# Query projection in two token halves, with each head's first selection behind its chunk, its low weight parts on GpSimd, and weight-matrix slots in tile order

## The chip, the core and the metric

One core of a Trainium2 chip runs the kernel as one program. The metric is device time in microseconds (us). The engines are PE (TensorE: matmuls), ACT (ScalarE: activations, copies out of PSUM), DVE (VectorE), POOL (GpSimd) and SP (SyncE, which only issues DMAs here). Each runs its own instruction list in order and meets the others at semaphores.

## The reference

A decoder layer for 512 tokens of width 1024. Only its last part, PEER (product-key expert retrieval), is touched. `hf` is the normed stream, 512 x 1024.

```python
q = (hf @ w_query).reshape(T, PEER_HEADS, 2, PEER_HALF)           # 8 heads, two halves of 128
s = jnp.einsum('thpd,pkd->thpk', q, sub_keys)                     # 128 sub-keys per half
sv, si = lax.top_k(s, PEER_TOPK)                                  # first selection: 16 of 128
cand = sv[..., 0, :, None] + sv[..., 1, None, :]                  # 16 x 16 sums
top_s, top_pos = lax.top_k(cand, PEER_TOPK)                       # second selection
idx = take_along_axis(cand_idx, top_pos)                          # 8 x 16 experts of 16384 per token
g = softmax(top_s)
out = sum over the 128 (t, k):  g * gelu(hf[t] . down[idx]) * up[idx]
```

The result, times a gate, is added to the stream and normed once more.

## The kernel before

All matmul weights arrive as chunks of 256 output columns (1 MB) in three raw slots. Each chunk is split into a high part (`whi`, ACT, `whi_make`) and a low part (`wlo`, raw minus high, DVE, `wlo_make` in `follow`), each in two buffers, and PE makes three products of 512 columns per k-tile: 48 matmuls per chunk. `CHUNKS` is the hand-written order. The last stage is `query`, eight chunks, one per head.

The PEER part serves its tokens in two ways. Token blocks 0 and 1 (`GB` = 2) **gather**: for each of 256 (block, k) pairs POOL issues an indirect DMA that brings one row of `down` per token (512 KB) into a ring, DVE multiplies it with `h2row` and sums (a **dot**, function `dots`; 256 of them, ring of 4), and later POOL gathers the rows of `up` and DVE adds them, scaled, to `accum` (a **sum**; 256, ring of 8). Token blocks 2 and 3 go **dense**: PE multiplies all 128 tiles of `downT` by the tokens (the **first stream**, `i` in `range(ET)`), ACT applies Gelu to each result and stores it in `wmat`; DVE and PE then build the gate matrix from one-hot vectors and multiply it into `wmat` (the **weighing**, 64 steps of `one_hots` and `weigh`); PE multiplies `wmat` by all 128 tiles of `up` (the **second stream**). SP feeds both streams through the ring `stream`.

DVE's own list sets the order of the rest. After the query stage it runs `route(n)` for the four token blocks: 16 first selections (`top16` over `s_all`), pairing, 8 second selections, decoding of positions with six 2048-wide one-hot operations. From block 1 on it mixes dots between these. Then, in this order:

```python
            for b in range(DB):
                softmax(GB + b).then_inc(pick_ready, 1)
            for b in range(GB):
                softmax(b)
            dots(P, P)
            dve.drain()
            dve.sem_inc(pre_ready, 1)
            dots(DOTS_FIRST)
```

`dots(P, P)` ends block 0's 128 dots, `DOTS_FIRST` more follow from block 1, and only then come the weighing, the remaining dots and the sums. `softmax(n)` waits for `exp_done`, which ACT gives in its loop over the first stream: at `i == EXP_AT` (100), behind the Gelu of 100 tiles, it makes the exponentials. The kernel after the last sum scales, norms and stores the output.

Of the kernel before, what the change touches and what calls it, by code (L numbers as in the profile page):

```python
# [26 lines left out]
SLOT0 = 18  # L27
# [5 lines left out]
DOTS_FIRST = 40  # L33
# [7 lines left out]
C_ID, C_ROT, C_MASK, C_FREQ, C_INV, C_IOTA, C_IOTAW = 0, 128, 256, 384, 385, 401, 529  # L41
C_W = 529 + 128
# [6 lines left out]
          ("gateB", 4), ("branchA", 4), ("out", 4), ("query", 8))  # L49
# [52 lines left out]

def tile_plan():


    tiles = []
    for s, c in CHUNKS:
        if (s, c) == ("query", 0):
            tiles += [("x1tok", n, "act") for n in range(8)]
        if (s, c) == ("query", 4):  # L110
            tiles += [("h2tok", n, "act") for n in range(2 * GB)]
            tiles += [("gaterow", n, "dve") for n in range(2)]
# [7 lines left out]
    tiles += [("score", n, "act") for n in range(16)]  # L120
    return tiles
# [25 lines left out]


def wslot(i):

    return (i + SLOT0) % ET


def layer(nc, consts, chans, rows, xT_d, pos_d, subk_d, ada_d, wdram, downT, down, up, x1d, gated, out):
# [4 lines left out]
    with ExitStack() as ctx:  # L159
# [85 lines left out]
        sq2 = place("sq2", [P, KT, S], f32, 164)  # L245
# [7 lines left out]
        q2T = place("q2T", [P, 2 * PH, S], f32, 68)  # L253

        wmat = place("wmat", [P, ET, DT], f32, 12)
        s_all = place("s_all", [P, TB, 2 * PH, NKEYS], f32, 100)
        s_left = place("s_left", [P, 2 * PH, NKEYS], f32, 132)
        cand_left = place("cand_left", [P, PH, PAIRS], f32, 132)
        onehot = place("onehot", [P, PH, TOPK, TOPK], f32, 12)
        at = [20.0]  # L260

        def scratch(name, shape, dt=f32, upto=30):
# [5 lines left out]
        top_v = scratch("top_v", [P, PH, 2, TOPK])  # L268
        top_i = scratch("top_i", [P, PH, 2, TOPK], u32)
        top_f = scratch("top_f", [P, PH, 2, TOPK])  # L270
# [5 lines left out]
        start_f = place("start_f", [P, 2, PH, TOPK], f32, 136)  # L276
# [6 lines left out]
        gate_row = place("gate_row", [P, D], f32, 192)  # L283
# [13 lines left out]
        x1stage = place("x1stage", [P, TB, D], f32, 164)  # L297
        x1tok = place("x1tok", [P, TB, D], f32, 30)
        yrow = place("yrow", [P, TB, D], f32, 46)
        gate_fin = place("gate_fin", [P, D], f32, 62)  # L300
        gain_row = place("gain_row", [P, D], f32, 66)
        junk = place("junk", [P, D], f32, 70)
# [51 lines left out]
        h2_ready = sem("h2_ready")  # L354
# [40 lines left out]
        N_OP = dict(norm1=0, pooled=8, ya=16, o=24, merged=32, norm2=40)  # L395
        N_MEAN = dict(norm1=0, norm2=1)
# [3 lines left out]
        def _(sp):  # L400
# [3 lines left out]
            for n, item in enumerate(STREAM):  # L404
                if n >= RAW_SLOTS:
                    sp.wait_ge(raw_free, n - RAW_SLOTS + 1)
# [9 lines left out]
                if item == ("w", FIRST["query"]):  # L416
                    sp.wait_ge(ada_done, 6)
                    sp.dma_start(bias_row[:, :], rows[:, D:2 * D]).then_inc(row_in, 16)
                if item == ("w", FIRST["query"] + 5):
# [6 lines left out]
            wait_emptied(sp, "gaterow", 1)  # L426
            sp.dma_start(gated, gate_row[:, :]).then_inc(gate_stored, 16)

            sp.wait_ge(x1_stored, 16)
            for n in range(2 * ET):  # L430
# [3 lines left out]
                sp.dma_start(stream[:, n % RING, :], src).then_inc(stream_in[n % RING], 16)  # L434
                if n == ET + 64:
                    sp.dma_start(x1tok[:, :, :], x1d).then_inc(fin_in, 16)
# [9 lines left out]
        def _(pe):  # L446
# [135 lines left out]

            t = 0
            for n, (stage, c) in enumerate(CHUNKS):
# [5 lines left out]
                if stage == "query" and c == 0:  # L590
                    norm2_mean()
                    t = tokens_first(t, x1T, range(8))
                if stage == "query" and c == 4:
                    pe.wait_ge(h2_ready, 8)
                    t = tokens_first(t, h2T, range(2 * GB))
                    for m in range(2):
                        free_bank(t)
                        pe.matmul(bank[:, BANK[t], :], ones[:, :], acc_ada[:, 1, m * S:(m + 1) * S],
                                  start=True, stop=True).then_inc(tile_ready, 1)
                        t += 1  # L600
                if c == 0:
                    ready = {"xp": "norm1", "pool": "pooled", "branchP": "ya",
                             "out": "merged", "query": "norm2"}.get(stage)
                    if ready:
# [4 lines left out]
                ah, al = {"pool": (r1_hi, r1_lo), "branchP": (ya_hi, ya_lo), "branchA": (r1_hi, r1_lo),  # L609
                          "query": (r1_hi, r1_lo)}.get(stage, (hT_hi, hT_lo))  # L610
# [21 lines left out]
                else:  # L632
                    for m in range(2):
                        free_bank(t)
                        for k in range(KT):
                            if WOVEN <= n < WOVEN_END and k % 4 == 0:
                                woven(4 * (n - WOVEN) - 12 + 2 * m + k // 4)
                            if stage == "branchA" and c == 0 and m == 0:
                                pe.wait_ge(alo_ready, N_OP["o"] + k + 1)
                            last = mm3(bank[:, BANK[t], :], wh[:, k, m * P:(m + 1) * P],  # L640
                                       wl[:, k, m * P:(m + 1) * P], ah[:, k, :], al[:, k, :],
                                       k == 0, k == KT - 1)
                        last.then_inc(tile_ready, 1)
                        t += 1

            for n in range(16):
                tb, g = n // 4, n % 4
                free_bank(t)
                if n == 0:
                    pe.wait_ge(pos_in, 48)  # L650
                    wait_emptied(pe, "query", 15)
                for j in range(4):
                    hp = 4 * g + j
                    last = pe.matmul(bank[:, BANK[t], j * P:(j + 1) * P], q2T[:, hp, tb * P:(tb + 1) * P],
                                     subk[:, hp % 2, :], start=True, stop=True)
                last.then_inc(tile_ready, 1)
                t += 1
# [38 lines left out]
            for i in range(ET):  # L696
                stream_tile(ET + i)
                for tb in range(DB):
                    for half in range(2):
                        last = pe.matmul(bank[:, 2 * tb + half, :], wmat[:, wslot(i), tb * P:(tb + 1) * P],  # L700
# [14 lines left out]
        def _(act):  # L715
# [137 lines left out]

            for n, (stage, c) in enumerate(CHUNKS):
# [30 lines left out]
                elif stage == "out":  # L885
                    if c == 3:
                        root(N_MEAN["norm2"], 1.0 / D)
                        for k in range(8):
                            act.activation(x1stage[:, k // 2, (k % 2) * S:(k % 2 + 1) * S],
                                           tile("x1tok", k), ACT.Copy).then_inc(act_emptied, 1)  # L890
                        for k in range(KT):
                            act.wait_ge(part_ready, 24 + k + 1)
                            act.activation(r1_hi[:, k, :], h2T[:, k, :], ACT.Identity,
                                           bias=modc[:, 24 + k:25 + k]).then_inc(ahi_ready, 1)
                elif stage == "query":
                    if c == 4:
                        for k in range(2 * GB):
                            act.activation(h2row[:, k // 2, (k % 2) * S:(k % 2 + 1) * S],
                                           tile("h2tok", k), ACT.Copy).then_inc(act_emptied, 1)
                    for m in range(2):  # L900
                        act.activation(q2T[:, 2 * c + m, :], tile(stage, 2 * c + m), ACT.Copy)\
                           .then_inc(act_emptied, 1)
            for n in range(16):
                tb, g = n // 4, n % 4
# [644 lines left out]
```

## Time and profile before

| quantity | value |
|---|---|
| median of 3 runs | 1987.07 us (1982.69 to 1989.71) |
| profiled execution: time / span of the core | 1997.52 / 1995.7 us |
| busy PE / DVE / ACT / POOL | 1633.1 / 1381.3 / 322.7 / 544.4 us |
| chain that ended last, share of the span | DVE 37%, DMA 30%, PE 22% |
| costliest lines of the chain | gathers of `down` 18%, gathers of `up` 10%, sums 10% |
| PE matmul of the first stream (L678) / second stream (L700) | 444.3 / 444.2 us busy |
| dots (L1269) / sums (L1428) on DVE | 311.6 / 328.8 us busy, 256 each |
| landing of a gather of `down` / of `up`, median | 7.4 / 7.1 us |
| bytes over the span | 489.76 MB, mean 245 GB/s |

PE has the most busy time, but its streams stand between stretches of DVE and gathers, so shares of the whole span do not say which one ends last; the stretches do.

### The profile page before, as it was taken

What the parts mean: (1) busy time and instruction counts of PE and PEld (TensorE: products, weight loads), DVE (VectorE), ACT (ScalarE), POOL (GpSimd) and SP (SyncE); (2) the same over time, 40 slices, a digit from 0 to 9 for tenths busy, and PEclk for the clock granted to TensorE, in tenths of its full rate; (3) what the DMA queues carried; (4) which work ended last, traced back from release to release, by engine and by line L of the source; (5) the groups of instructions that cost most, each with busy time, mean ns of one, the idle gap of its engine ahead of it and who ended that gap; (6) DMA issues with size and microseconds to landing.
All of it is one profiled execution on the core that took longest, in us unless ns stands there. A gap on an engine that the chain in (4) does not pass through costs nothing.

```text
span 1995.7 us, 18994 instructions
## 1 busy us (share of the span) xinstructions
PE 1633.1 (82%) x6668; PEld 1191.1 (60%) x6668; DVE 1381.3 (69%) x2790; ACT 322.7 (16%) x658; POOL 544.4 (27%) x516
## 2 busy tenths in 40 slices
PE   2798999989997999999999967789999899980000
PEld 1686877767776788888888866654444344430000
DVE  5656456666554268899888579985555566679998
ACT  2242244436413221111111100000000000000001
POOL 0000000000000003353444420014444544457773
PEclk7899999989998999999999986669999899995555
DMA  7323311132423228999998960019999999999995
GB/s 292 140 92 147 127 64 64 64 127 106 169 95 106 74 72 311 356 365 375 353 369 322 386 253 0 1 52 392 376 374 375 412 409 409 410 409 388 367 384 230
DMA packets 123070, 489.76 MB, mean 245 GB/s; under 512 B 13792, under 2 KB 14048, under 8 KB 113632
## 3 DMA queue, kind: packets, MB, share of 16 engines
q0 software_dynamic: 73728, 268.47, 35.2%
q1 hardware_dynamic: 49248, 220.09, 29.3%
q8 instruction: 53, 0.87, 0.2%
q14 instruction: 41, 0.34, 0.1%
HBM read 483.78 MB, written 4.72 MB: 245 GB/s over the span
## 4 chain that ended last, share of the span: by engine, by line
DVE 37%; DMA 30%; PE 22%; issue 3%; DVEq 3%; ACT 2%; POOL 2%; SPq 0%; ACTq 0%; POOLq 0%
DMA ring<-in_down,idx 18%; DMA ring<-in_up,idx 10%; DVE accum L1428 10%; PE bank L449 6%; PE bank L450 6%; PE bank L451 6%; DVE ring L1269 6%; DVE h2T L1398 3%; DVE h2T L1397 2%; DVE wmat L1408 2%; POOL ring L1453 2%; DVE acc_ada L956 1%; DMA raw<-in_ada 1%; DVE onehot L1352 1%; PE bank L535 1%
## 5 line engine op out<-in xcount | busy, mean ns | idle before, releaser
L1453 POOL DMA_INDIRECT ring<-in_down,idx x256 | 278.8, 1089 | 1249.8 <-DVE idx L1360 759.7
L700 PE MATMUL bank<-stream,wmat 128*128 128x512 f32 x1024 | 444.2, 597 | 9.1 <-DMA stream<-in_up 8.3
L678 PE MATMUL bank<-h2T,stream 128*128 128x256 f32 x2048 | 444.3, 380 | 2.6 <-ACT wmat L930 2.6
L1269 DVE CUSTOM_DVE_ANT_0 ring<-ring,h2row 128x1024 f32<-128x1024 f32 x256 | 311.6, 1222 | 167.2 <-DMA ring<-in_down,idx 164.1
L678 PEld LDWEIGHTS bank<-h2T,stream 128*128 128x128 f32 x2048 | 390.1, 191 | 56.2 <-issue 3.0
L1428 DVE SCALAR_TENSOR_TENSOR accum<-ring,share,accum 128x1024 f32<-128x1024 f32 x256 | 328.8, 1284 | 107.6 <-DMA ring<-in_up,idx 94.1
L700 PEld LDWEIGHTS bank<-stream,wmat 128*128 128x128 f32 x1024 | 196.0, 192 | 256.7 <-issue 246.5
L1453 POOL DMA_INDIRECT ring<-in_up,idx x256 | 265.4, 1037 | 172.5 <-DVE accum L1428 119.2
L449 PE MATMUL bank<-hT_hi,whi 128*128 128x512 f32 x384 | 160.9, 419 | 23.5 <-DVE hT_lo L1006 17.0
L975 DVE TENSOR_TENSOR wlo<-raw,whi 128x2048 fp32r<-128x2048 f32 x45 | 103.0, 2290 | 108.4 <-ACT whi L722 108.0
L690 PE MATMUL bank<-h2T 128*128 128x128 f32 x512 | 114.1, 393 | 49.9 <-DVE h2T L1398 49.9
L450 PE MATMUL bank<-hT_lo,whi 128*128 128x512 f32 x384 | 153.0, 398 | 0.0
L451 PE MATMUL bank<-hT_hi,wlo 128*128 128x512 f32 x384 | 152.4, 397 | 0.0
L690 PEld LDWEIGHTS bank<-h2T 128*128 128x128 f32 x512 | 97.8, 285 | 66.4 <-DVE h2T L1398 66.3
L930 ACT ACTIVATE wmat<-bank 128x256 f32<-128x256 f32 x128 | 49.0, 384 | 392.2 <-PE bank L678 383.7
L449 PEld LDWEIGHTS bank<-hT_hi,whi 128*128 128x128 f32 x384 | 74.0, 193 | 42.0 <-DVE hT_lo L1006 17.1
L722 ACT ACTIVATE whi<-raw 128x2048 fp32r<-128x2048 f32 x45 | 86.1, 1912 | 79.8 <-PE bank L451 68.9
L449 PE MATMUL bank<-r_hi,whi 128*128 128x512 f32 x208 | 83.5, 402 | 18.3 <-DVE r_lo L1006 10.0
L450 PEld LDWEIGHTS bank<-hT_lo,whi 128*128 128x128 f32 x384 | 74.2, 193 | 17.2 <-issue 2.9
L1398 DVE TENSOR_SCALAR h2T<-cst,ijT,gT 128x128 f32<-128x128 f32 x256 | 84.3, 329 | 0.0
L451 PEld LDWEIGHTS bank<-hT_hi,wlo 128*128 128x128 f32 x384 | 74.1, 193 | 16.4
L450 PE MATMUL bank<-r_lo,whi 128*128 128x512 f32 x208 | 82.7, 397 | 0.0
(201 smaller groups left out, 1596.8 us busy)
## 6 DMA issues: line engine op xcount, KB each, us to landing
stream<-in_downT SPq DMA_DIRECT2D x128, 512.0 KB, 6.5
stream<-in_up SPq DMA_DIRECT2D x128, 512.0 KB, 6.8
raw<-in_ada SPq DMA_DIRECT2D x24, 1024.0 KB, 6.0
raw<-in_w_query SPq DMA_DIRECT2D x8, 1024.0 KB, 4.9
raw<-in_w_xp SPq DMA_DIRECT2D x4, 1024.0 KB, 6.0
raw<-in_w_gateA SPq DMA_DIRECT2D x4, 1024.0 KB, 4.9
raw<-in_w_branchP SPq DMA_DIRECT2D x4, 1024.0 KB, 4.8
raw<-in_w_q SPq DMA_DIRECT2D x4, 1024.0 KB, 4.8
```

What stands on the lines that cost most here:

```text
L449: pe.matmul(dst, lhi, rhi, start=first, stop=False)
L450: pe.matmul(dst, lhi, rlo, start=False, stop=False)
L451: return pe.matmul(dst, llo, rhi, start=False, stop=last)
L678: last = pe.matmul(bank[:, 4 + i % 2, 0:DT], stream[:, i % RING, k * P:(k + 1) * P], h2T[:, k, GB * P:S], start=(k == 0), stop=(k == KT - 1))
L690: last = pe.matmul(bank[:, 6 + par, n * P:(n + 1) * P], h2T[:, 4 * par + n, 0:P], h2T[:, 4 * par + n, P:2 * P], start=True, stop=True)
L700: last = pe.matmul(bank[:, 2 * tb + half, :], wmat[:, wslot(i), tb * P:(tb + 1) * P], stream[:, (ET + i) % RING, half * S:(half + 1) * S], ...
L722: act.activation(whi[:, n % 2], raw_w(n), ACT.Copy).then_inc(hi_ready, 1)
L975: dve.tensor_tensor(wlo[:, n % 2], raw_w(n), whi[:, n % 2].bitcast(f32), ALU.subtract)\
L1269: dve.tensor_tensor_reduce(out=ring[g % RING][:, :], in0=ring[g % RING][:, :], in1=h2row[:, b, :], scale=1.0, scalar=0.0, op0=ALU.mult, op ...
L1398: last = dve.tensor_scalar(h2T[:, 4 * par + n, P:2 * P], iota_w, ijT[:, b, 0, t:t + 1], gT[:, b, t:t + 1], ALU.is_equal, ALU.mult)
L1428: dve.scalar_tensor_tensor(accum[:, b, :], ring[slot][:, :], share[:, b, k:k + 1], accum[:, b, :], ALU.mult, ALU.add).then_inc(sum_done, 1)
L1453: pool.indirect_dma_start(out=ring[slot][:, :], out_offset=None, in_=table, in_offset=bass.IndirectOffsetOnAxis(ap=idx[:, b, k:k + 1], axi ...
```

## The change

The query stage becomes two stages, `queryA` (tokens 0 to 255) and `queryB` (256 to 511), of eight chunks each; each loads and splits the same eight weight chunks again. A matmul has 256 columns instead of 512. The scores of a head follow one chunk later (`score`), ACT copies them out, and DVE makes that head's first selection (`stage1`: 2 token blocks x 2 halves). Pairing, second selection and decoding of a token block are `stage2`. The low parts of these 16 chunks are made by POOL, in its list ahead of all gathers. The second norm is made in halves, with the shift on ACT; transposes for the stored stream and the gate row move into the `out` stage and between the chunks. `q2T` now holds two heads, `s_all` one half's scores. `wmat` is filled in tile order (`wslot` goes), `DOTS_FIRST` goes from 40 to 64, and the dots mixed into the routing are dealt by `fill`, one per 1.4 us of credit.

```diff
-DOTS_FIRST = 40
+DOTS_FIRST = 64
+ROUTE_PER_DOT = 1.4
-          ("gateB", 4), ("branchA", 4), ("out", 4), ("query", 8))
+          ("gateB", 4), ("branchA", 4), ("out", 4), ("queryA", 8), ("queryB", 8))
...
+            def score(t, u):
+                c = u % 8
+                free_bank(t)
...
+                wait_emptied(pe, "queryB" if u >= 8 else "queryA", 2 * c + 1)
+                for tb in range(2):
+                    for m in range(2):
+                        last = pe.matmul(bank[:, BANK[t], (2 * tb + m) * P:(2 * tb + m + 1) * P],
+                                         q2T[:, c % 2, m, tb * P:(tb + 1) * P], subk[:, m, :],
...
+            def shifted(half):
+                toks = slice(half * HT, (half + 1) * HT)
+                for k in range(KT):
+                    act.wait_ge(part_ready, 24 + half * KT + k + 1)
+                    act.activation(hT_hi[:, k, toks], h2T[:, k, toks], ACT.Identity, bias=modc[:, 24 + k:25 + k])
+                    act.activation(h2T[:, k, toks], h2T[:, k, toks], ACT.Identity,
+                                   bias=modc[:, 24 + k:25 + k]).then_inc(ahi_ready, 1)
...
                 if i == PICK_AT + 1:
                     for b in range(DB):
                         pick_out(b)
-                if 70 <= i < 70 + 8 * TB and i % 8 == 6:
-                    act.wait_ge(logit_ready, (i - 70) // 8 + 1)
-                if i == 102:
-                    act.wait_ge(pick_ready, DB)
+                if i == 88:
+                    act.wait_ge(routes_done, 1)
...
-                if n >= len(CHUNKS):
+                if n >= QUERY:
                     return
                 wlo_make(n)
...
+            def fill(us):
+
+                credit[0] += us
+                while credit[0] >= ROUTE_PER_DOT:
+                    credit[0] -= ROUTE_PER_DOT
+                    dots(1, P)
...
-            for n in range(TB):
-                for g in range(4):
-                    wait_emptied(dve, "score", 4 * n + g)
-                route(n, 1 if n else 0)
+            for c in range(PH):
+                stage1(0, c, nothing)
+            stage2(0, nothing)
+            stage2(1, fill)
+            for c in range(PH):
+                stage1(1, c, fill)
+            for n in range(GB, TB):
+                stage2(n, fill)
+            dve.sem_inc(routes_done, 1)
...
-            pool.wait_ge(gate_stored, 16)
+            for n in range(QUERY, len(CHUNKS)):
+                pool.wait_ge(lo_ready, n)
+                pool.wait_ge(hi_ready, n + 1)
+                pool.tensor_tensor(wlo[:, n % 2].rearrange("p a b -> p (a b)"),
+                                   raw_w(n).rearrange("p a b -> p (a b)"),
+                                   whi[:, n % 2].bitcast(f32).rearrange("p a b -> p (a b)"), ALU.subtract)\
+                    .then_inc(lo_ready, 1)
+                pool.drain()
+                pool.sem_inc(qraw_free, 1)
+
+            pool.wait_ge(x1_stored, 16)
```

POOL's list before, from the first gather on:

```order
L1453 DMA ring<-in_down,idx 128x1024 [waits idx_ready,gate_stored]
L1453 DMA ring<-in_down,idx 128x1024 x3
L1453 DMA ring<-in_down,idx 128x1024 [waits dot_done] x124
L1453 DMA ring<-in_down,idx 128x1024 [waits dot_done,idx_ready]
L1453 DMA ring<-in_down,idx 128x1024 [waits dot_done] x127
```

and after:

```order
L1553 TENSOR_TENSOR wlo<-raw,whi 128x2048 [waits hi_ready,lo_ready] x16
L1545 DMA ring<-in_down,idx 128x1024 [waits idx_ready,x1_stored]
L1545 DMA ring<-in_down,idx 128x1024 x3
L1545 DMA ring<-in_down,idx 128x1024 [waits dot_done] x124
L1545 DMA ring<-in_down,idx 128x1024 [waits dot_done,idx_ready]
```

Sixteen subtractions now stand ahead of the first gather, each behind its chunk's high part.

ACT's list from the end of the query stage to the copies of the picks (`ijT`), before; `wmat` is a Gelu of the first stream, `share` and `picked` are the exponentials:

```order
L901 ACTIVATE q2T<-bank 128x512 [waits tile_ready] x4
L905 ACTIVATE s_all<-bank 128x512 [waits tile_ready] x16
L930 ACT_TABLE_LOAD
L930 ACTIVATE wmat<-bank 128x256 [waits tile_used] x70
L930 ACTIVATE wmat<-bank 128x256 [waits tile_used,logit_ready]
...
L911 ACT_TABLE_LOAD
L911 ACTIVATE share<-share 128x128 [waits logit_ready] x2
L911 ACTIVATE picked<-picked 128x128 [waits logit_ready] x2
L930 ACT_TABLE_LOAD
L930 ACTIVATE wmat<-bank 128x256 [waits tile_used] x2
L930 ACTIVATE wmat<-bank 128x256 [waits tile_used,pick_ready]
```

and after:

```order
L959 ACTIVATE q2T<-bank 128x256 [waits tile_ready] x2
L906 ACTIVATE s_all<-bank 128x512 [waits s1_done,tile_ready] x2
L985 ACT_TABLE_LOAD
L985 ACTIVATE wmat<-bank 128x256 [waits tile_used] x88
L985 ACTIVATE wmat<-bank 128x256 [waits tile_used,routes_done]
L985 ACTIVATE wmat<-bank 128x256 [waits tile_used] x11
L968 ACT_TABLE_LOAD
L968 ACTIVATE share<-share 128x128 [waits logit_ready] x2
L968 ACTIVATE picked<-picked 128x128 [waits logit_ready] x2
L985 ACT_TABLE_LOAD
L985 ACTIVATE wmat<-bank 128x256 [waits tile_used] x9
```

The exponentials keep their place behind 100 Gelus; the wait on the routing stands at tile 88, and the one on `pick_ready` behind them is gone.

On DVE the dots can be counted in the two lists (one `ring,pre<-ring,h2row` each): before, 126 stand ahead of the first softmax and 42 between the softmaxes and the weighing; after, 89 and 103. The dots behind the weighing go from 88 to 64.

## Rows read from the trace of the kernel before

**Rows 1.** View of windows, all engines, from the first gather to the end.

```profile
core 0: us, PE busy (x) PEld busy (x) DVE busy (x) ACT busy (x) POOL busy (x), PEclk, DMA share, GB/s
...
760.00:1080.00 320.00, 320.00 (x1485) 281.69 (x1484) 281.98 (x906) 38.68 (x98) 142.05 (x129) 1.00 0.96 360
...
1178.00:1334.00 156.00, 114.23 (x513) 97.90 (x513) 153.94 (x575) 0.00 (x0) 1.46 (x2) 0.65 0.03 8
...
1786.00:1990.00 204.00, 0.41 (x1) 0.00 (x0) 187.98 (x149) 6.18 (x10) 140.70 (x131) 0.51 0.90 346
```

**Rows 2.** Timeline of ACT (ScalarE) around its hundredth weight tile.

```profile
1067.22 0.38 ACT L930 ACTIVATE wmat<-bank 128x256 f32<-128x256 f32 x1 [3.07 <-PE bank L678]
...
1069.84 1.28 ACT L930 ACT_TABLE_LOAD   x1
```

**Rows 3.** Timeline of DVE (VectorE) at the end of the routing.

```profile
1081.28 0.28 DVE L1368 TENSOR_REDUCE expsum<-picked 128x8 f32<-128x128 f32 x1
...
1084.63 1.22 DVE L1269 CUSTOM_DVE_ANT_0 ring<-ring,h2row 128x1024 f32<-128x1024 f32 x1
```

**Rows 4.** Timeline of DVE where the weighing begins.

```profile
1176.49 1.23 DVE L1269 CUSTOM_DVE_ANT_0 ring<-ring,h2row 128x1024 f32<-128x1024 f32 x1 [0.20 <-DMA ring<-in_down,idx]
...
1177.64 0.28 DVE L1397 TENSOR_SCALAR h2T<-cst,ijT 128x128 f32<-128x128 f32 x1
```

**Rows 5.** View of windows, instructions on the gather ring alone.

```profile
1080.00:1178.00 98.00, 52.53 (x43) 42.59 (x43) 0.96 0.97 367
1334.00:1440.00 106.00, 57.28 (x47) 51.83 (x46) 0.99 0.95 361
1548.00:1786.00 238.00, 146.60 (x115) 113.07 (x117) 0.98 1.03 410
```

**Rows 6.** Timeline of DVE just after the last matmul of the weight stream.

```profile
1783.07 17.81 DVE L1428 SCALAR_TENSOR_TENSOR accum<-ring,share,accum 128x1024 f32<-128x1024 f32 x13
```

**Rows 7.** View of DMA issues from 1790 to 1974, us to landing.

```profile
ring<-in_up,idx POOLq DMA_INDIRECT x128, 6.0
```

**Rows 8.** Timeline of PE (TensorE), two neighbouring matmuls of 256 columns.

```profile
304.08 0.28 PE L451 MATMUL bank<-whi,hT_lo 128*128 128x256 f32 x1
304.20 0.28 PE L449 MATMUL bank<-whi,hT_hi 128*128 128x256 f32 x1
```

**Rows 9.** Timeline of PE before and after the score matmuls.

```profile
707.32 14.53 PE L654 MATMUL bank<-subk,q2T 128*128 128x128 f32 x128 [0.78 <-ACT q2T L901]
721.68 4.48 PE L678 MATMUL bank<-h2T,stream 128*128 128x256 f32 x20
```

**Rows 10.** Timeline of ACT in the query projection.

```profile
607.48 1.92 ACT L722 ACTIVATE whi<-raw 128x2048 fp32r<-128x2048 f32 x1
619.96 0.60 ACT L901 ACTIVATE q2T<-bank 128x512 f32<-128x512 f32 x1 [10.57 <-PE bank L451]
```

**Rows 11.** Timeline of DVE from the second norm into the query projection.

```profile
597.70 3.35 DVE L997 RECIPROCAL rms<-rms 128x512 f32<-128x512 f32 x1 [1.89 <-ACT rms L733]
601.12 5.39 DVE L1243 SCALAR_TENSOR_TENSOR h2T<-x1T,scaleF,rms 128x512 f32<-128x512 f32 x8
...
627.84 2.29 DVE L975 TENSOR_TENSOR wlo<-raw,whi 128x2048 fp32r<-128x2048 f32 x1 [10.66 <-ACT whi L722]
```

**Rows 12.** Timeline of DVE in the first routing.

```profile
711.89 3.19 DVE L1278 MAX8 top_v<-s_all 128x8 f32<-128x128 f32 x16 [22.35 <-ACT s_all L905]
...
731.30 0.29 DVE L1337 CAST top_f<-top_i 128x256 f32<-128x256 uint32 x1
...
758.92 0.29 DVE L1360 SCALAR_TENSOR_TENSOR idx<-rowij 128x128 int32<-128x128 f32 x1
```

**Rows 13.** Timeline of POOL (GpSimd), gathers of `down`.

```profile
760.13 1.07 POOL L1453 DMA_INDIRECT ring<-in_down,idx  x1 [759.68 <-DVE idx L1360]
...
843.75 1.68 POOL L1453 DMA_INDIRECT ring<-in_down,idx  x1 [7.63 <-DVE pre L1269]
...
850.43 0.94 POOL L1453 DMA_INDIRECT ring<-in_down,idx  x1 [0.30 <-issue]
```

More of the change, by code:

```diff
@@ L26 @@
 ET = 128
-SLOT0 = 18
 RING = 4
@@ L32 @@
 PICK_AT = 108
-DOTS_FIRST = 40
+DOTS_FIRST = 64
+ROUTE_PER_WLO = 4.0
+ROUTE_PER_DOT = 1.4
+HALF = {"queryA": 0, "queryB": 1}
+HT = S // 2
 NEG = -3.0e38
@@ L107, in tile_plan @@
     for s, c in CHUNKS:
-        if (s, c) == ("query", 0):
-            tiles += [("x1tok", n, "act") for n in range(8)]
-        if (s, c) == ("query", 4):
+        if (s, c) == ("out", 1):
+            tiles += [("gaterow", n, "dve") for n in range(2)]
+        if (s, c) == ("out", 3):
+            tiles += [("x1tok", 2 * n, "act") for n in range(4)]
+        if (s, c) == ("queryA", 1):
+            tiles += [("x1tok", 2 * n + 1, "act") for n in range(4)]
+        if (s, c) == ("queryA", 3):
             tiles += [("h2tok", n, "act") for n in range(2 * GB)]
-            tiles += [("gaterow", n, "dve") for n in range(2)]
         if s == "pool":
@@ L119, in tile_plan @@
             tiles += [(s, 2 * c + n, who) for n in range(2)]
-    tiles += [("score", n, "act") for n in range(16)]
+        if s in HALF and (s, c) != ("queryA", 0):
+            tiles.append(("score",) + score_before(s, c) + ("act",))
+    tiles.append(("score", 15, "act"))
     return tiles
@@ L589, in _ @@
                         o_columns(h)
[L590 to L595, printed above, removed]
+                if (stage, c) == ("out", 1):
                     for m in range(2):
                         free_bank(t)
+                        if m == 0:
+                            pe.wait_ge(ada_acc, 6)
                         pe.matmul(bank[:, BANK[t], :], ones[:, :], acc_ada[:, 1, m * S:(m + 1) * S],
@@ L644, in _ @@
                         t += 1
[L646 to L657, printed above, removed]
+                    if stage in HALF and (stage, c) != ("queryA", 0):
+                        t = score(t, *score_before(stage, c))
+            t = score(t, 15)
             def stream_tile(n):
@@ L699, in _ @@
                     for half in range(2):
-                        last = pe.matmul(bank[:, 2 * tb + half, :], wmat[:, wslot(i), tb * P:(tb + 1) * P],
+                        last = pe.matmul(bank[:, 2 * tb + half, :], wmat[:, i, tb * P:(tb + 1) * P],
                                          stream[:, (ET + i) % RING, half * S:(half + 1) * S],
@@ L884, in _ @@
                         act.activation(hT_hi[:, i, :], tmpo[:, i, :], ACT.Copy).then_inc(ahi_ready, 1)
[L885 to L896, printed above, removed]
+                elif stage == "out" and c == 3:
+                    for k in range(0, 8, 2):
+                        x1_out(k)
+                    root(N_MEAN["norm2"], 1.0 / D)
+                    shifted(0)
+                elif stage in HALF:
+                    if (stage, c) == ("queryA", 1):
+                        shifted(1)
+                        for k in range(1, 8, 2):
+                            x1_out(k)
+                    if (stage, c) == ("queryA", 3):
                         for k in range(2 * GB):
+                            if k == 0:
+                                act.wait_ge(part_ready, 24 + 2 * KT)
                             act.activation(h2row[:, k // 2, (k % 2) * S:(k % 2 + 1) * S],
@@ L900, in _ @@
                     for m in range(2):
-                        act.activation(q2T[:, 2 * c + m, :], tile(stage, 2 * c + m), ACT.Copy)\
+                        if c >= 2 or stage == "queryB":
+                            act.wait_ge(tile_ready, TILE_AT["score", 8 * HALF[stage] + c - 2] + 1)
+                        act.activation(q2T[:, c % 2, m, :], tile(stage, 2 * c + m)[:, 0:HT], ACT.Copy)\
                            .then_inc(act_emptied, 1)
-            for n in range(16):
-                tb, g = n // 4, n % 4
-                act.activation(s_all[:, tb, 4 * g:4 * g + 4, :].rearrange("p a b -> p (a b)"),
-                               tile("score", n), ACT.Copy).then_inc(act_emptied, 1)
+                    if (stage, c) != ("queryA", 0):
+                        score_out(*score_before(stage, c))
+            score_out(15)
             def exponentials(n):
@@ L1279, in top16 @@
                     if n % 4 == 3:
-                        dots(among)
+                        fill(0.8)
                 dve.drain()
```

226 lines of the change are left out of this document (140 added, 86 removed).

## The prediction, made before the changed kernel ran

> **What bounds the kernel now.** I read the view of windows first [rows 1]. From 760 to 1080 PE and the gathers run together, and the DMA engines are 96% busy at 360 GB/s; so it goes on to 1178 [rows 5]. From 1178 to 1334 only the weighing runs: DVE is busy 153.94 of 156 us, the DMA engines rest at 0.03, PE has a mean granted clock of 0.65. PE's last matmul ends near 1786, and 204 us of sums and output follow in which PE does nothing. So the end is set by DVE's own list, and PE matters only through where the weighing starts, since the second stream follows it. Then I read what DVE does at three places. Its softmaxes begin at 1081.28 and the next dot at 1084.63 [rows 3]. ACT has its hundredth Gelu at 1067.22 and goes back to Gelu at 1069.84, with the exponentials made [rows 2]. So the routing ended some 11 us after its exponentials: DVE did not wait for them. The weighing begins at 1177.64 [rows 4], after 42 more dots.
>
> **The rates.** Beside a stream the ring of 4 gives 43 dots in 98 us, 2.28 each, and 47 records in 106 us after the weighing, 2.26 each [rows 5]; I take 2.3 there. Sums beside the stream: 115 in 238 us, 2.07 each [rows 5]. With the stream over: 13 sums in 17.81 us, 1.37 each [rows 6]. PE's stream: first matmul at 721.68 [rows 9], hundredth Gelu at 1067.22 [rows 2], so 3.455 us a tile and 442 us for 128.
>
> **The change, part by part.**
>
> *Query stage.* Two matmuls of 256 columns are 0.12 us apart [rows 8], so a chunk takes 48 x 0.12 = 5.8 us. The 64 score matmuls took 14.53 us [rows 9], four are 0.9. PE alone would need 6.7 us a chunk. But the splitting makes a loop over two chunks: when a chunk's matmuls end, ACT has to copy its queries and, once the four score matmuls are through (0.9), the scores (0.6, as a copy of 512 columns [rows 10]; with wakes 0.8), then makes the high part (1.92 [rows 10]), POOL makes the low part (P), and the matmuls of the chunk after next follow (5.8). Period (0.9 + 0.8 + 1.9 + 0.3 + P + 5.8) / 2 = (9.7 + P) / 2.
>
> *P.* No POOL arithmetic is in the trace. DVE needs 2.29 us for the same subtraction [rows 11], which is the lower end, and there PE's 6.7 is the period. POOL's own instructions stretch from 0.94 to 1.68 us when DVE is at work [rows 13]. I take twice the DVE time, 4.6, a period of 7.15; for the upper end four times, 9.2, a period of 9.45. The Trainium skill, GPSIMD Engine Reference, section "Elementwise — side-by-side cycle accounting", gives 4497 ns for this size on GpSimd against 2293 on VectorE; the trace agrees with the second, the first would make the period 7.1 and move nothing.
>
> *Start.* Half the transposes of the stored stream (16) and the two gate-row products move ahead of the norm: at 0.23 us each, and four times that for 512 columns, 5.4 us. The reciprocal that began at 597.70 [rows 11] begins at 603.1; its half takes 1.7, the first part 0.34, and ACT then makes two 256-column results per k-tile, 0.38 each (as in [rows 2]), so chunk 0 ends at about 614.6. Chunk 1 needs banks that ACT frees only after two high parts, 16 shifts of 0.38 and a copy: about 624, end 629.8. Chunk 2 ends at 636.5, chunk 3, behind four row copies, at 646.4. Twelve more at 7.15 end at 732, and after the last scores the first stream starts at 734, against 721.68: **12 us late**.
>
> *First gather.* `idx` of block 0: the scores of head 7 of the first half come out at about 684; 16 first selections took 711.89 to 731.30, so four take 4.85, and the rest of a route took 731.30 to 758.92 plus 0.3 [rows 12], 27.9. That gives 717. But POOL does its sixteenth subtraction first, done when the last chunk's matmuls start, 726. The gather starts there, **34 us sooner** than 760.13 [rows 13]. The stored stream's DMA, issued in `queryA`, is long done. DVE meets its first mixed dot right after 717 and waits for it till 733.
>
> *Routing.* Before, three routes with 42 dots each filled 1081.3 - 760.1 = 321 us, 107 each; less 19.4 + 27.9 of routing that is 1.42 us per mixed dot. After: three second stages of 27.9, eight first ones of 4.85, 89 dots of 1.42: 249 us. Routing ends at 982.
>
> *The wait that is new.* The exponentials still stand behind 100 Gelus: 734 + 345.5 + 2.6 = 1082. So DVE, which reached them 11 us late, comes **100 us early** and stands still with four gathered rows in the ring. Behind the waiting softmax stand 103 dots, where 42 stood, then the weighing, and behind that PE's second stream, and the last 64 dots and all sums. `DOTS_FIRST` = 64 adds 24 of these dots, and the thinner mixing 37.
>
> *Start of the weighing.* Softmaxes end at 1086, the first stream at 734 + 442 = 1176. In these 90 us go 4 ready dots (5 us) and 85 / 2.28 = 37. The other 62 have the DMA engines to themselves. Their price isn't in the trace. Lower end: DVE's own spacing, 1.15 us, from 1176.49 to 1177.64 [rows 4]; upper end: 2.28. With the ring of 8 and no stream a gather landed in 6.0 us [rows 7], queued behind seven others, at 1.37 a sum; with 4 in flight the round (issue 1.2, landing 4 to 5, dot 1.2) gives about 1.6. I take 1.6: 99 us. The weighing starts at 1275, against 1177.6: **97 us late**. Its own 156 us and PE's stream keep their lengths, so PE ends 97 us late too.
>
> *After it.* 24 fewer dots at 2.3 give 55 us back. In these, 55 / 2.07 = 27 more sums are made before PE ends, and each spares 1.37 us behind it: 37 us back. The slots of `wmat` and the one iota instead of two change no instruction and no size in the weighing: nothing.
>
> *Sum.* The span 1995.7 + 97 - 37 = 2056. The profiled execution's time was 1997.52, 10.4 above the median of 1987.07; so against the median, 1987 + 60 = **2047**.
>
> **A rule weighed.** POOL's gather instruction took 1.68 us instead of 0.94 at 843.75 [rows 13], while DVE worked on two-input operations. The Trainium skill, GPSIMD Engine Reference, section "Key points", says that POOL shares its SBUF interfaces with VectorE and contends with instructions that have two SBUF inputs. By that rule the low parts beside DVE's decoding (about 14 us of one-hot work in `queryB`) would take longer, some 5 us in all; without it, none.
>
> **The rivals.**
> 1. *The wait costs more: the dots keep their price.* If the ring of 4, not the stream, sets 2.28, the 62 dots cost 141 us, and the time is 2089. For it: landing was still 6.0 us without a stream [rows 7]. Against: DVE took 1.37 per sum there. 12%.
> 2. *POOL becomes the bound of the query stage.* At P = 9.2, twelve periods of 9.45 instead of 7.15 delay everything by 28 us: 2075. For it: the stretch in [rows 13]; against: DVE mostly waits or has one-input selections in that stage. 13%.
> 3. *The other side: faster.* The dots behind the softmax run at DVE's own pace. From 1086, 103 at 1.15 end at 1204; the weighing is then 27 us late, the 37 given back outweigh it: 1977. It decides from 1214 on, that is 1.24 us a dot. Against: beside the stream two stretches gave 2.28 and 2.26 [rows 5], with the DMA engines at 97%; this needs both to be wrong. 4%.
> 4. *The change doesn't do what it says:* the early selection gains nothing, because the first gather waits for POOL's queue till 760 as before. The routing would then end at 1016, still before 1082, and the time would be the same 2047. It is no case of its own; it shows how little the early start is worth while 1082 stands.
>
> **How the numbers follow.** Main case 71%, with its own range from all 62 dots at 1.15 (2019) to 2.28 less a little (2080). Rivals 1 and 2 make 25% between 2065 and 2095, rival 3 4%. The range 2015 to 2092 leaves out rival 3 and the sum of rivals 1 and 2. 0.3% (6 us) is about what this measurement can tell from no change. Faster 4%; within 0.3% needs 1.3 us a dot in all stretches, 2%; slower 94%.
>
> **What would show it.** In the profile after: first stream at about 734, first gather near 726, last mixed dot near 980; then DVE idle for some 100 us, put down to ACT's exponentials (or a DMA); PE idle between 1176 and 1275, DMA lighter there, granted clock down; weighing 156 us long; PE's end near 1883; then about 110 sums at 1.37. Wrong would be: a softmax that starts with no wait before it, or a PE gap below 40 us ahead of the weighing.

## The result, and the profile after

The changed kernel takes 2081.38 us (median of 4 runs, 2075.61 to 2082.82), against 1988.39 for the kernel before: ratio 1.0468, 95% interval 1.0438 to 1.0498. It is 93 us slower. The ratios here and below leave out slow executions; the only one, 3378.58 us, is among e9's twelve, whose median without it is 1990.36. The profiled execution of the changed kernel has a span of 2080.3 us, 84.6 more than the span before.

The view of windows, all engines; the cuts are the end of the routing, the end of the first stream and the weighing:

```profile
core 0: us, PE busy (x) PEld busy (x) DVE busy (x) ACT busy (x) POOL busy (x), PEclk, DMA share, GB/s
740.00:988.00 248.00, 248.00 (x1151) 218.86 (x1150) 221.43 (x705) 28.69 (x73) 113.52 (x92) 1.00 0.95 343
988.00:1088.00 100.00, 100.00 (x465) 88.26 (x464) 0.80 (x5) 13.91 (x35) 0.94 (x1) 1.00 0.48 169
1088.00:1183.00 95.00, 94.13 (x440) 82.74 (x438) 51.39 (x90) 12.57 (x34) 44.06 (x39) 1.00 0.95 355
1183.00:1307.00 124.00, 3.09 (x14) 3.07 (x15) 82.42 (x145) 0.00 (x0) 79.17 (x64) 0.51 0.83 282
1307.00:1463.00 156.00, 118.32 (x507) 99.20 (x507) 154.06 (x564) 0.00 (x0) 1.32 (x1) 0.63 0.00 1
```

Two stretches have no counterpart in [rows 1, 5]. From 988 to 1088 DVE is busy for 0.80 us of 100, and the DMA engines fall to 0.48, since no gather is asked for. From 1183 to 1307 PE is busy for 3.09 us of 124. The weighing behind them has kept its length. The view of waits names the first stretch, and PE's second:

```profile
DVE ring L1327 <- DMA ring<-in_down,idx: 162.1, 156, 4.2
PE bank L721 <- DVE h2T L1490: 158.7, 63, 121.8
DVE expsum L1455 <- ACT picked L968: 99.1, 1, 99.1
```

Each line gives the total us, how often, and the longest single wait: DVE waited once, 99.1 us, for ACT's exponentials (`picked`), and PE's longest wait, 121.8 of its 158.7 us, was for the one-hot vectors that DVE makes at the start of the weighing. Against [rows 2, 3], the timelines of ACT and DVE around the exponentials and at the weighing:

```profile
1084.82 0.39 ACT L985 ACTIVATE wmat<-bank 128x256 f32<-128x256 f32 x1 [3.07 <-PE bank L709]
...
1087.44 1.28 ACT L985 ACT_TABLE_LOAD   x1
```

```profile
986.97 1.22 DVE L1327 CUSTOM_DVE_ANT_0 ring<-ring,h2row 128x1024 f32<-128x1024 f32 x1
...
1087.25 0.28 DVE L1455 TENSOR_REDUCE expsum<-picked 128x8 f32<-128x128 f32 x1 [99.05 <-ACT picked L968]
...
1300.80 1.23 DVE L1327 CUSTOM_DVE_ANT_0 ring<-ring,h2row 128x1024 f32<-128x1024 f32 x1 [0.22 <-DMA ring<-in_down,idx]
1301.95 0.28 DVE L1489 TENSOR_SCALAR h2T<-cst,ijT 128x128 f32<-128x128 f32 x1
```

The last mixed dot begins at 986.97, the softmax at 1087.25, the weighing at 1301.95, 124 us behind [rows 4].

The view of windows on the gather ring alone, in the three stretches with dots and the last one with sums (the columns are DVE's dots or sums, then POOL's gathers, then clock, DMA share and GB/s):

```profile
740.00:988.00 248.00, 107.13 (x89) 113.52 (x92) 1.00 0.95 343
1088.00:1183.00 95.00, 48.92 (x40) 44.06 (x39) 1.00 0.95 355
1183.00:1305.00 122.00, 77.31 (x63) 79.17 (x64) 0.51 0.83 281
...
1900.00:2060.00 160.00, 145.91 (x114) 114.92 (x107) 0.55 0.96 368
```

63 dots with no stream beside them took the 119 us from 1183 to 1302: 1.89 each. The DMA view gives 5.6 us from issue to landing there.

The start of the gathers, POOL and DVE:

```profile
712.71 4.69 POOL L1553 TENSOR_TENSOR wlo<-raw,whi 128x2048 fp32r<-128x2048 f32 x1 [2.74 <-ACT whi L753]
719.54 4.83 POOL L1553 TENSOR_TENSOR wlo<-raw,whi 128x2048 fp32r<-128x2048 f32 x1 [2.14 <-ACT whi L753]
726.96 4.60 POOL L1553 TENSOR_TENSOR wlo<-raw,whi 128x2048 fp32r<-128x2048 f32 x1 [2.59 <-ACT whi L753]
740.07 1.10 POOL L1545 DMA_INDIRECT ring<-in_down,idx  x1 [8.51 <-DVE idx L1447]
```

```profile
705.59 4.47 DVE L1399 TENSOR_SCALAR best_f<-best_sh 128x128 f32<-128x128 uint32 x1
...
713.03 4.52 DVE L1412 TENSOR_TENSOR best_f<-best_f,start_f 128x128 f32<-128x128 f32 x1
717.62 2.29 DVE L1434 TENSOR_TENSOR h2T<-best_f,cst 128x2048 f32<-128x2048 f32 x1
719.99 6.53 DVE L1439 TENSOR_TENSOR h2T<-h2T,top_f 128x2048 f32<-128x2048 f32 x1
726.59 2.29 DVE L1443 TENSOR_REDUCE rowij<-h2T 128x128 f32<-128x2048 f32 x1
728.95 4.76 DVE L1434 TENSOR_TENSOR h2T<-best_f,cst 128x2048 f32<-128x2048 f32 x1
...
738.86 0.29 DVE L1447 SCALAR_TENSOR_TENSOR idx<-rowij 128x128 int32<-128x128 f32 x1
```

Read the two together. The operation at 719.99 takes 2.29 us where no subtraction of POOL runs (e6 below shows the same line of the kernel); here it ends at 726.52, 2.15 after POOL's subtraction from 719.54 to 724.37 has ended. The subtraction of 128 columns at 713.03 ends at 717.55, behind POOL's at 717.40. The reduction at 726.59 runs beside POOL's next subtraction, from 726.96 on, and isn't held. So block 0's second stage, from 694.77 to 739.15, took 44.4 us instead of 27.9.

### The profile page after: what moved, and what is told of

Read it like the earlier page. It is cut to its first block, busy times and chain, and to the rows that moved or that the text cites. A ratio compares the mean times of both kernels' runs of the same rounds, so it can differ in the third digit from the quotient of the medians.

```text
span 2080.3 us, 19998 instructions
## 1 busy us (share of the span) xinstructions
PE 1641.8 (79%) x7052; PEld 1216.5 (58%) x7052; DVE 1393.2 (67%) x2791; ACT 347.6 (17%) x706; POOL 643.2 (31%) x532
## 4 chain that ended last, share of the span: by engine, by line
PE 39%; DVE 25%; DMA 25%; POOL 4%; issue 3%; ACT 3%; DVEq 2%; SPq 0%; ACTq 0%; POOLq 0%
PE bank L709 17%; DMA ring<-in_down,idx 12%; DMA ring<-in_up,idx 12%; DVE accum L1520 8%; PE bank L463 6%; PE bank L464 6%; PE bank L465 6%; POOL ring L1545 4%; DVE h2T L1490 3%; DVE h2T L1489 2%; DVE ring L1327 2%; DVE wmat L1500 2%; DVE acc_ada L1011 1%; DMA raw<-in_ada 1%; ACT whi L753 1%
## 5 line engine op out<-in xcount | busy, mean ns | idle before, releaser
L1545 POOL DMA_INDIRECT ring<-in_down,idx x256 | 298.7, 1167 | 563.4 <-DVE pre L1327 530.6
L1553 POOL TENSOR_TENSOR wlo<-raw,whi 128x2048 fp32r<-128x2048 f32 x16 | 74.2, 4639 | 656.9 <-ACT whi L753 656.9
L463 PE MATMUL bank<-hT_hi,whi 128*128 128x512 f32 (+1 forms) x640 | 237.2, 371 | 46.0 <-DVE hT_lo L1061 17.0
L721 PE MATMUL bank<-h2T 128*128 128x128 f32 x512 | 116.7, 400 | 158.7 <-DVE h2T L1490 158.7
L464 PE MATMUL bank<-hT_lo,whi 128*128 128x512 f32 (+1 forms) x640 | 226.9, 355 | 0.0
L465 PE MATMUL bank<-hT_hi,wlo 128*128 128x512 f32 (+1 forms) x640 | 226.8, 354 | 0.0
L463 PEld LDWEIGHTS bank<-hT_hi,whi 128*128 128x128 f32 x640 | 125.3, 196 | 67.2 <-issue 29.5
L464 PEld LDWEIGHTS bank<-hT_lo,whi 128*128 128x128 f32 x640 | 125.3, 196 | 17.1 <-issue 3.1
L465 PEld LDWEIGHTS bank<-hT_hi,wlo 128*128 128x128 f32 x640 | 124.8, 195 | 16.2
L1030 DVE TENSOR_TENSOR wlo<-raw,whi 128x2048 fp32r<-128x2048 f32 x37 | 84.7, 2290 | 51.2 <-ACT whi L753 50.9
L753 ACT ACTIVATE whi<-raw 128x2048 fp32r<-128x2048 f32 x53 | 101.2, 1910 | 82.4 <-PE bank L465 70.6
```

The lines of the kernel that those rows point to most:

```text
L463: pe.matmul(dst, lhi, rhi, start=first, stop=False)
L464: pe.matmul(dst, lhi, rlo, start=False, stop=False)
L465: return pe.matmul(dst, llo, rhi, start=False, stop=last)
L721: last = pe.matmul(bank[:, 6 + par, n * P:(n + 1) * P], h2T[:, 4 * par + n, 0:P], h2T[:, 4 * par + n, P:2 * P], start=True, stop=True)
L753: act.activation(whi[:, n % 2], raw_w(n), ACT.Copy).then_inc(hi_ready, 1)
L1030: dve.tensor_tensor(wlo[:, n % 2], raw_w(n), whi[:, n % 2].bitcast(f32), ALU.subtract)\
```

## The experiments

The question for the first four: is the 99 us wait the loss, or the number of dots ahead of the weighing, or the query stage itself? e5 prices the dots in the gap, e6, e8 and e10 ask what POOL's subtractions do, e7 and e9 whether the change can pay at all. Each ratio is to the kernel before on the same chip.

**e1: the exponentials earlier.** In the changed kernel:

```diff
-EXP_AT = 100
-PICK_AT = 108
+EXP_AT = 72
+PICK_AT = 80
```

> Changed kernel, exponentials behind 72 Gelus instead of 100 (picks at 80). Wait theory: the routing ends at 988, so the softmaxes run at about 991 instead of 1087 and DVE no longer stands still for 99 us; with 4 ready dots, then one per 2.4 us beside the stream, about 80 of the 103 dots are done when the first stream ends at 1182, 23 more at 1.93 put the weighing at 1226 instead of 1302: 76 us faster, about 2005 us. Rival, the dots' amount is what costs and the wait is idle time off the path: under 10 us faster, about 2075 us. Rival, the query stage: no change at all.

Measured: 1998.34 us, ratio 1.0051 (1.0034 to 1.0068), 83 us faster than the changed kernel's median. The softmax begins at 991.23 after a wait of 4.4, the weighing at 1217.3:

```profile
DVE expsum L1455 <- ACT picked L968: 4.4, 1, 4.4
```

The two numbers that set the place of the exponentials explain nearly the whole 93 us. The two rivals fall.

**e2: and fewer dots ahead of the weighing.** As e1, and:

```diff
-DOTS_FIRST = 64
+DOTS_FIRST = 44
```

> As the run before, and DOTS_FIRST 44 instead of 64. Wait theory: 83 dots stand behind the softmax, the weighing starts at about 1188 with no gap on PE, and 20 more dots stand behind it at about 1.55 us each in the end: about 1998 us, 7 us under the run before. If the wait was not the cause, the 20 dots fewer give 20 x 1.93 - 31 = 8 us on top of what the changed kernel has, about 2073 us.

Measured: 1989.11 us, ratio 0.9996 (0.9976 to 1.0016). The weighing begins at 1180.6, and in the ring's windows 83 dots stand beside the stream at 2.31 each:

```profile
990.00:1182.00 192.00, 101.54 (x83) 85.76 (x83) 1.00 0.99 376
```

83 us of the 93 came back in e1, and these fewer dots bring the rest: with these constants the change is worth neither a gain nor a loss.

**e3: `DOTS_FIRST` alone, in the kernel before.**

```diff
-DOTS_FIRST = 40
+DOTS_FIRST = 64
```

> Kernel before, DOTS_FIRST 64 instead of 40 alone. Wait theory: this is a small part. 24 more dots at 1.93 us while PE is idle put the weighing 46 us later, and 24 fewer behind it give 37 us back: about 9 us slower than before, 1997 us. Rival, DOTS_FIRST explains the whole loss: 93 us slower, about 2081 us.

Measured: 1996.17 us, ratio 1.0036 (1.0019 to 1.0053), 7 us slower. That part of the change costs a few us, not ninety.

**e4: PE's gap taken out, DVE's wait left in.** In the changed kernel:

```diff
-DOTS_FIRST = 64
+DOTS_FIRST = 3
```

> Changed kernel, DOTS_FIRST 3 instead of 64, so that 42 dots stand between softmax and weighing as in the kernel before; the exponentials stay at 100. The weighing would start at about 1186, with no gap on PE, 116 us earlier; but 61 more dots stand behind it, at 1.55 us each 95 us: about 2059 us, 22 us faster. So the 99 us of waiting would be seen to be lost even where PE never waits. Rival, PE's gap of 122 us is the loss itself: about 1965 us.

Measured: 2052.61 us, ratio 1.0319 (1.0283 to 1.0356). The weighing starts at 1184.7 and PE's gap is gone, but only 29 of the 93 us come back; DVE still waits 95.5 us. This tells the seen gap from its cause: a PE gap of 122 us can be closed for a quarter of its length, because the dots that were not made in DVE's 99 idle us have to be made somewhere. With 42 dots behind the softmax, as before the change, and the wait left in, the kernel still loses 63 us.

**e5: the price of a dot with no stream beside it.** In the changed kernel `DOTS_FIRST` 104 instead of 64.

> Changed kernel, DOTS_FIRST 104 instead of 64: 40 more dots in the gap in which no stream runs. It measures the price of a dot there over 103 of them. If the 1.93 us of the changed kernel's 63 dots is the ring's own price, the weighing starts 77 us later, at 1379, and 40 fewer dots behind it give 62 us back: about 2096 us. If the price was that high only at the start of the gap and 1.6 us holds later, the weighing starts at 1366 and the time is about 2083 us.

Measured: 2096.96 us, ratio 1.0551 (1.0517 to 1.0584); weighing at 1376.7, 74.8 us later for 40 dots, 1.87 each. The ring's windows in the gap:

```profile
1190.00:1290.00 100.00, 64.76 (x54) 67.44 (x53) 0.50 0.82 272
1290.00:1370.00 80.00, 52.81 (x43) 53.91 (x43) 0.50 0.83 275
```

1.85 and 1.86 in the two parts: the price holds over the whole gap, so it isn't that of its start, and the DMA engines are not full at it (0.83). That it is set by the ring's depth of 4 is argued from this; no run changed the depth.

**e6: POOL's subtractions short.** In the changed kernel POOL makes 128 of 2048 columns of each low part of the query stage and the rest of the buffer keeps older values, so the time isn't that of the whole computation:

```diff
-                pool.tensor_tensor(wlo[:, n % 2].rearrange("p a b -> p (a b)"),
+                pool.tensor_tensor(wlo[:, n % 2].rearrange("p a b -> p (a b)")[:, 0:128],
...
```

> Changed kernel; POOL makes only the first 128 of 2048 columns of the 16 low weight parts of the query stage, the rest of the buffers stays as an older chunk left it. Theory that a POOL subtraction holds up two-input operations of DVE until it ends: the second stage of block 0 takes 28 us instead of 44.5, the eight products of the second half norm take 3.3 us instead of 11.7, block 0's indices are ready at about 712 instead of 739, the query period falls from 7.15 to 6.7 us and the first stream starts at 727 instead of 739. The time falls only by the 12 us of the stream, to about 2069 us, because the exponentials still stand behind 100 tiles. Rival, DVE was slow there for another reason (PSUM, DMA traffic): the second stage still takes over 40 us, and only the period gains, about 2075 us.

Measured: 2072.03 us, ratio 1.0422 (1.0395 to 1.0448). DVE's timeline:

```profile
614.93 3.26 DVE L1309 SCALAR_TENSOR_TENSOR h2T<-x1T,scaleF,rms 128x256 f32<-128x256 f32 x8
```

```profile
692.16 0.29 DVE L1418 CAST top_f<-top_i 128x256 f32<-128x256 uint32 x1
...
708.39 2.29 DVE L1439 TENSOR_TENSOR h2T<-h2T,top_f 128x2048 f32<-128x2048 f32 x1
...
720.57 0.29 DVE L1447 SCALAR_TENSOR_TENSOR idx<-rowij 128x128 int32<-128x128 f32 x1
```

The eight products take 3.26 us (11.66 in the changed kernel), the second stage 28.7 us (44.4). POOL's instructions did hold DVE. The first stream starts at 733.12 instead of 739.28 and the weighing at 1293.7 instead of 1301.95; the spans differ by 8.0 us. The indices, ready 18 us sooner, only lengthen DVE's wait for the exponentials, from 99 to 109.8 us, because these still stand behind 100 tiles. Single executions differ by a few us ahead of this stage: the eight products begin at 614.93 here and at 611.03 in e8, which is the same program up to there.

**e7: a denser mix.** In the changed kernel:

```diff
-EXP_AT = 100
-PICK_AT = 108
-DOTS_FIRST = 64
-ROUTE_PER_DOT = 1.4
+EXP_AT = 86
+PICK_AT = 94
+DOTS_FIRST = 57
+ROUTE_PER_DOT = 1.0
```

> Changed kernel with one dot per 1.0 us of credit (125 dots in the routing instead of 89), exponentials at 86, picks at 94, DOTS_FIRST 57. With 1.42 us for a mixed dot the routing ends at 1039, when the 86th Gelu is done; 60 dots stand behind the softmax and the weighing starts at about 1183 with 71 dots behind it: about 1973 us, 15 us faster than the kernel before. If the early selection is worth nothing even so, it comes out at 1988 or above.

Measured: 1985.43 us, ratio 0.9989 (0.9966 to 1.0012): no difference from the kernel before, and 12 us above what was expected. ACT's timeline:

```profile
1058.74 0.66 ACT L985 ACTIVATE wmat<-bank 128x256 f32<-128x256 f32 x2 [14.31 <-DVEq L1470]
```

The routing ended at 1060 and not at 1039: a mixed dot cost (1060.4 - 739.5 - 121.6) / 125 = 1.59 us. ACT, which may not overwrite the routing's scratch with tile 88 before that, stood 14.31 us, and the first stream ended 11 us later than in the changed kernel. The weighing began at 1195.0 instead of 1183. ACT's stall isn't shown to be the whole of that: DVE ended its last dot at 1195.0 too, having waited for its gather, since the later routing had pushed its 60 dots back as well. The stretch of the routing in the view of windows:

```profile
739.50:1060.40 320.90, 312.54 (x1449) 274.85 (x1448) 266.05 (x780) 40.07 (x99) 155.91 (x128) 0.99 0.96 356
```

These 125 dots and the routing left to do took 320.9 us. Before, 126 dots and 20 us more of routing took 321 us, with DVE busy for 281.98 of the 320 us in [rows 1] and 266.05 here, and the DMA share was 0.96 in both. DVE had less to do and waited longer for gathers, 43.7 us in all against 29.8.

**e8: as e7, with POOL's subtractions short** (the same part left out as in e6).

> As the run before, and POOL makes only 128 of 2048 columns of the query stage's low parts (the rest stays as an older chunk left it). It bounds what POOL's subtractions cost once the exponentials are in place: the stream starts 12 us earlier and the first gather 20 us or more, so about 10 more dots are done by the end of the first stream and wait for the exponentials at 86 instead: 12 to 20 us under the run before, about 1957 us. Under 5 us would say that POOL's part in the time is small.

Measured: 1960.8 us, ratio 0.9878 (0.9845 to 0.9911), 25 us under e7. Indices at 716.1, routing ended at 1034.4, weighing at 1167.9. The routing's stretch again took 2.55 us a dot (125 in 318.3 us); it only began sooner. Once the exponentials stand in the right place, POOL's subtractions cost up to 25 us; in e6 leaving them out was worth 9. This counts two things together that no run separates in full: their own length in the loop over the chunks, and their holding of DVE.

**e9: all constants in place.** `ROUTE_PER_DOT` 1.2 (104 mixed dots), `EXP_AT` 81, `PICK_AT` 89, `DOTS_FIRST` 43.

> Changed kernel with one dot per 1.2 us of credit (104 in the routing), exponentials at 81, picks at 89, DOTS_FIRST 43: everything placed so that neither DVE waits for the exponentials nor ACT for the routing. Theory that the gathers beside the stream run at a fixed 2.3 us each whatever the order of dots and routing: 171 dots before the weighing, as with the exponentials at 72 and DOTS_FIRST 44 (172), the weighing at about 1185, and the time that of that run, 1989 us, the same as the kernel before. Rival, denser mixing lets DVE work off more: 10 us or more below the kernel before.

Measured: 1990.87 us, ratio 1.0002 (0.9989 to 1.0014), the same as the kernel before. In the profiled execution the softmax waited 10.4 us, where no wait was planned. The first one-hot vectors of the weighing were made at 1175.8, 5 us sooner than in e2, but PE's first matmul on them began at 1183.31, when the first stream had ended, and the last one-hot began at 1333.2, as in e2 (1333.1). So here the stream's end set the weighing and not the dots.

**e10: as e9, POOL's subtraction in four pieces.**

```diff
+                for c0 in range(0, KT * CH, 512):
+                    last = pool.tensor_tensor(wlo[:, n % 2].rearrange("p a b -> p (a b)")[:, c0:c0 + 512],
...
+                last.then_inc(lo_ready, 1)
```

> As the run before, and POOL makes each low part in four pieces of 512 columns. Theory that a two-input operation of DVE waits for the POOL instruction under way, not for POOL's work as a whole: no DVE operation of block 0's second stage is held longer than one piece, about 1.3 us, the stage takes about 33 us instead of 44.5 and the indices are ready at about 729 instead of 739. The pieces cost POOL some 0.6 us a chunk, the period rises to about 7.4 and the stream starts 3 to 4 us later; the sum is 0 to 5 us faster. Rival, DVE is held for the whole of POOL's work: the stage still takes 44 us or more.

Measured: 1994.41 us, ratio 1.0033 (1.0017 to 1.0049), 3.5 us slower than e9. But the mechanism is in the timelines of DVE and POOL:

```profile
703.87 1.25 DVE L1399 TENSOR_SCALAR best_f<-best_sh 128x128 f32<-128x128 uint32 x1
...
713.61 3.23 DVE L1439 TENSOR_TENSOR h2T<-h2T,top_f 128x2048 f32<-128x2048 f32 x1
```

```profile
703.74 5.13 POOL L1554 TENSOR_TENSOR wlo<-raw,whi 128x512 fp32r<-128x512 f32 x4 [1.73 <-ACT whi L753]
711.58 8.84 POOL L1554 TENSOR_TENSOR wlo<-raw,whi 128x512 fp32r<-128x512 f32 x4 [2.70 <-ACT whi L753]
```

The held `TENSOR_SCALAR` took 1.25 us, one piece, and not 4.47; the second stage 36.9 us (692.75 to 729.64). In return POOL waits for DVE: its four pieces took 8.84 us. The indices were ready 11 us sooner than in e9, but the first gather, behind POOL's last pieces, came at 738.14 instead of 741.42, 3 us sooner, and the first stream began at 745.29 instead of 740.63. That these 5 us make the loss is argued, not shown by itself.

## Why the prediction was right, step by step

The direction and the mechanism held, and 2081 lies in 2015 to 2092. The number, 2047, was 34 us short: 60 us of loss were forecast and 93 measured. 2081 is also 1 us above the main case's own range (2019 to 2080). It lies in the stretch that was given to rivals 1 and 2, though POOL's time and the dots' price were not theirs, so that the range held owes something to them. By its own steps:

- **Query stage.** P was taken as 4.6 us; the 16 subtractions took a median of 4.608. The period came out at 7.09, in ACT's copies of the queries (12 chunks in 85 us), where 7.15 was forecast; so rival 2 (P of 9.2) fell. The first stream was to start at 734 and starts at 739.28. The start-up term was too small: the eight products of the second half norm took 11.66 us, where half of the 5.39 us of [rows 11] is 2.7, because two POOL subtractions held them; e6 shows it (3.26 us).
- **First gather.** 726 was predicted, from POOL's queue; it came at 740.07, and it was DVE's indices that were late (the row says 8.51 us of waiting for `idx`). The step "the rest of a route, 27.9" failed: 44.4 us, again POOL's holding. "A rule weighed" had looked at the same contention from the wrong side: it let POOL's work be stretched (by 5 us), and took DVE as untouched.
- **Routing.** End at 982 predicted, 988 measured; 1.42 us per mixed dot held (89 dots in 248 us, less 121.6 of routing: three second stages of 27.6 and eight first ones of 4.85 by [rows 12]). At 125 dots it was 1.59 (e7).
- **The new wait.** 100 us predicted, 99.05 measured; 103 dots behind it as counted. e1 shows that this is most of the loss, 83 of 93 us.
- **Dots with no stream: the mis-sized term.** 62 at 1.6 us were predicted, 99 us; 63 took 119, 1.89 each. Landing was assumed at 4 to 5 us with four gathers in flight, which by the prediction's own sum gives 1.6 to 1.85, and the lower end was taken; landing was 5.6. Four dots took 4 x 1.89 = 7.6 us, of which landing and the dot's own 1.2 are 6.8. e5 confirmed the price over 97 dots. The term is 20 of the weighing's 27 us of error; the stream's start, 5 us late, is another 5. Rival 1 (2.28) priced it too high by about 0.4 us a dot, the main case (1.6) too low by 0.3. Rival 3 needed 1.24 and fell.
- **Behind the weighing.** 37 us were to come back; 818.1 us from the start of the weighing to the end became 778.4, 39.7.
- **Rival 4** was said to be no case of its own. e6 bears it out: with indices 18 us sooner the span fell by 8.0 us, about what the sooner stream and weighing give (6.2 and 8.3 us), while tile 100 stood.

The sum: 124.3 - 39.7 = 84.6 us of span, where 97 - 37 = 60 was forecast. The medians are 93 us apart, 8 us more than the spans of the two profiled executions, since the profiled execution of the kernel before lay above the median of its runs (1997.52 against 1987.07) and the one after hardly did (2082.82 against 2081.38). That the 10 us above the median would recur in both was a silent assumption; it makes up the rest of the 34 us and is no step of the mechanism.

Why didn't the early selection pay even in e2 and e9? The traces show three things. The first gather comes at 740 instead of 760, but the first stream starts at 739 instead of 722, and the weighing can't start before that stream ends (e9): its last matmul begins at 1168.7 before and at 1182.1 in e2. A dot beside a stream costs 2.2 to 2.3 us in either kernel, so 172 dots fit ahead of the weighing in e2, 168 before, and the weighing begins 3 us later. And where dots are mixed densely into the routing, they and the routing take 2.55 us a dot before, in e7 and in e8, so routing taken out of that stretch doesn't shorten it. That these cancel the lead of 20 us is argued from the three, not shown by a run of its own. A version with the low parts off POOL, and complete, was not tried, so whether it would keep e8's 25 us is open.

## What to carry to other kernels

A step that is tied to another engine's progress by a constant ("behind tile 100") is a due time; whoever moves the work ahead of it has to move the constant, and has to count what is queued behind the waiting instruction, since both the wait and that count enter the loss: with the wait gone and 103 dots kept the loss was 10 us (e1), with 42 dots and the wait kept 63 (e4). A gap on the busiest engine is not its own cause: closing it by reordering gave back 29 us (e4), removing the wait behind it 83 (e1). Before moving arithmetic to GpSimd, list VectorE's two-input operations, and its one-input `TENSOR_SCALAR` and `CAST`, that will run beside it: here such an operation could wait for the end of a whole GpSimd instruction of 4.6 us.

## What the hardware showed that was not expected

DVE operations with two SBUF inputs, and `TENSOR_SCALAR` and `CAST` of one input, waited for the POOL subtraction under way to end: 4.52 us instead of 0.29, 6.53 instead of 2.29, 4.47 instead of 0.23, 1.07 instead of 0.29. `MAX8`, `FIND_INDEX8`, `MATCH_REPLACE8` and `TENSOR_REDUCE` beside the same subtractions kept their 0.28 and 2.29 us (0.22 to 0.23 for 72 columns). Not every `CAST` beside a subtraction waited: one of 128 columns that began at 705.29, just behind POOL's start at 705.26, kept its 0.22 us. With POOL's work cut into four instructions the wait shrank to one piece, 1.25 us, and POOL waited for DVE in its turn (8.84 us for 5.1). The Trainium skill, SBUF — State Buffer, section "Terms", says of the port pair shared by the two engines that it is exclusive, "held for the full instruction", and that the loser blocks; this case's traces agree in both directions, with the numbers above. The Trainium skill's 4497 ns for an add of this size on GpSimd (GPSIMD Engine Reference, section "Elementwise — side-by-side cycle accounting") stands beside a median of 4608 ns for the subtraction here.

A gather of 512 KB with at most four in flight and nothing else on the DMA engines landed after 5.6 us (DMA share 0.83), hardly sooner than the 6.0 with a ring of eight [rows 7] (0.96 in the same kind of stretch after the change). So fewer transfers in flight hardly shortened the landing, and the ring of 4 gave 1.85 to 1.89 us a dot where the ring of 8 gave 1.37 us a sum. Whether a deeper ring would make the dots cheaper was not tried.
